# A row of norm factors by two DMA steps over memory instead of two transposes and a copy, in three of four feed-forward parts

## The reference

```
def rmsnorm(x, gain):
    y = xf * lax.rsqrt(jnp.mean(xf * xf, axis=-1, keepdims=True) + EPS)
    return y * gain
def swiglu(x, w_gate, w_up, w_down):
    return (jax.nn.silu(x @ w_gate) * (x @ w_up)) @ w_down

for l in range(2):
    x = x + 0.5 * swiglu(rmsnorm(x, ffn1_norm[l]), ffn1_w_gate[l], ffn1_w_up[l], ffn1_w_down[l])
    x = x + token_mixing(rmsnorm(x, mix_norm[l]), ...)      # three attention branches, gates, w_out
    x = x + 0.5 * swiglu(rmsnorm(x, ffn2_norm[l]), ffn2_w_gate[l], ffn2_w_up[l], ffn2_w_down[l])
```

## Time and profile before

| | us |
|---|---|
| median of 3 runs | 1146.28 (1145.64 to 1146.29) |
| profiled execution, its own time | 1145.91 |
| its span | 1144.1 |
| PE busy | 1136.0 (99%) |
| DVE busy | 777.6 (68%) |
| ACT busy | 638.4 (56%) |
| POOL busy | 70.0 (6%) |

### The profile page before, as it was taken

The page is one execution under the profiler, slowest core; times in us unless marked ns, Lnnn a source line. Parts: engine busy times, 40 slices in busy tenths (PEclk is TensorE's granted clock), DMA queues, the critical chain, the costliest instruction groups (busy, mean ns, idle before and its releaser), DMA issues.

```text
span 1144.1 us, 16114 instructions
## 1 busy us (share of the span) xinstructions
PE 1136.0 (99%) x5963; PEld 962.9 (84%) x5963; DVE 777.6 (68%) x1054; ACT 638.4 (56%) x942; POOL 70.0 (6%) x79
## 2 busy tenths in 40 slices
PE   8999999999999999999999999999999999999998
PEld 6888888888778888888888888888877788888887
DVE  4776656778677676566676756668677695766655
ACT  6545545656783565455555545556577745555542
POOL 3020000211000000000020200002110000000000
PEclk9999999999999999999999999999999999999999
DMA  9956554555354665555566556536445545656620
GB/s 310 307 192 202 183 186 146 175 170 172 124 170 148 221 221 184 185 194 197 174 166 236 184 184 190 194 99 217 148 149 161 207 142 189 222 189 196 193 85 37
DMA packets 138364, 207.34 MB, mean 181 GB/s; under 512 B 6818, under 2 KB 99028, under 8 KB 138292
## 3 DMA queue, kind: packets, MB, share of 16 engines
q1 hardware_dynamic: 137444, 205.55, 54.8%
q0 software_dynamic: 752, 0.79, 0.9%
q10 hardware_dynamic: 96, 0.02, 0.0%
HBM read 205.29 MB, written 1.05 MB: 180 GB/s over the span
## 4 chain that ended last, share of the span: by engine, by line
PE 95%; DVE 2%; ACT 1%; DMA 1%; DVEq 1%; issue 0%; SPq 0%; ACTq 0%
PE bank L526 27%; PE bank L493 16%; PE bank L497 16%; PE bank L496 16%; PE bank L530 15%; PE bank L507 1%; PE bank L720 1%; DMA raw<-in_ffn_w_up 1%; ACT probs L1018 1%; PE bank L693 1%; PE bank L741 1%; PE bank L709 0%; PE bank L708 0%; DVE w_low L1118 0%; DVE probs L1329 0%
## 5 line engine op out<-in xcount | busy, mean ns | idle before, releaser
L1118 DVE TENSOR_TENSOR w_low<-raw,w_high 128x1024 fp32r<-128x1024 f32 x388 | 472.3, 1236 | 281.6 <-ACT w_high L869 281.3
L869 ACT ACTIVATE w_high<-raw 128x1024 fp32r<-128x1024 f32 x388 | 402.0, 1055 | 317.5 <-PE bank L493 112.4
L526 PE MATMUL bank<-xT,w_high 128*128 128x512 f32 x1392 | 339.8, 391 | 0.2 <-DVE xT L1136 0.2
L526 PEld LDWEIGHTS bank<-xT,w_high 128*128 128x128 f32 x1392 | 255.4, 188 | 49.7 <-DVE xT L1136 0.7
L530 PEld LDWEIGHTS bank<-xT,w_low 128*128 128x128 f32 x1408 | 180.9, 191 | 7.4 <-issue 0.6
L530 PE MATMUL bank<-xT,w_low 128*128 128x256 f32 x1408 | 185.1, 283 | 0.4 <-DVE w_low L1118 0.4
L493 PE MATMUL bank<-w_high,xT 128*128 128x512 f32 (+1 forms) x448 | 174.4, 389 | 0.2
L497 PE MATMUL bank<-w_low,xT 128*128 128x512 f32 (+1 forms) x448 | 171.3, 382 | 0.0
L496 PE MATMUL bank<-w_high,xT 128*128 128x512 f32 (+1 forms) x448 | 171.1, 382 | 0.0
L493 PE MATMUL bank<-w_high,oT_high 128*128 128x512 f32 x416 | 162.3, 390 | 0.0
L497 PE MATMUL bank<-w_low,oT_high 128*128 128x512 f32 x416 | 161.9, 389 | 0.0
(11 more groups left out here) (129 smaller groups left out, 743.8 us busy)
## 6 DMA issues: line engine op xcount, KB each, us to landing
raw<-in_w_in SPq DMA_DIRECT2D x92, 512.0 KB, 4.5
raw<-in_ffn_w_down SPq DMA_DIRECT2D x88, 512.0 KB, 4.2
raw<-in_ffn_w_gate SPq DMA_DIRECT2D x87, 512.0 KB, 4.1
raw<-in_ffn_w_up SPq DMA_DIRECT2D x87, 512.0 KB, 5.0
raw<-in_w_out SPq DMA_DIRECT2D x16, 512.0 KB, 4.4
raw<-in_w_branch_c SPq DMA_DIRECT2D x8, 512.0 KB, 4.1
raw<-in_w_branch_a SPq DMA_DIRECT2D x4, 512.0 KB, 3.9
raw<-in_w_branch_b SPq DMA_DIRECT2D x4, 512.0 KB, 6.0
```

Source lines behind the costliest of these rows:

```text
L526: return nc.tensor.matmul(bank[b0 + n][:, :], w_high[:, slot, column(k, n)], xT[:, k], start=k == 0, stop=k == KB - 1)
L869: act.activation(w_high[:, slot], raw[:, in_slot, (p % 2) * 1024:(p % 2) * 1024 + 1024], ACT.Copy).then_inc(sem["high_ready"], 1)
L1118: dve.tensor_tensor(w_low[:, slot], raw[:, FILL_SLOT[p // 2], (p % 2) * 1024:(p % 2) * 1024 + 1024], w_high[:, slot].bitcast(F32), ALU.sub ...
```

## The change

In the first feed-forward part of the first layer nothing changes (it is called cold; its semaphores have other names). In the other three, PE makes no transposes of the factors and has no wait for the row. ACT instead sends the two columns of norm_scale, 128 values of 4 bytes each, to a line of 256 values in device memory (`send_line`, two DMAs, at the start of `ffn_chunks`, after a wait for norm_ready), and later (`send_row`, at the place of copy_row) waits for both to land and loads the line 128 times, once into each partition, as `norm_row` (128 KB in all). DVE waits for that DMA before `scale_gate` of the part's first chunk.

```diff
--- before.py
+++ after.py
@@ -100,7 +100,7 @@
     "pair_used": PAIRS, "high_ready": PAIRS, "low_ready": PAIRS,
     "blocks_turned": 18, "blocks_high": 18, "blocks_low": 18,
     "gate_done": 2 * CHUNKS, "gate_up_done": 2 * CHUNKS, "gate_summed": 2 * CHUNKS, "gate_scaled": 2 * CHUNKS, "silu_ready": 2 * CHUNKS, "hidden_ready": 2 * CHUNKS,
-    "hidden_high": 2 * CHUNKS, "hidden_low": 2 * CHUNKS, "up_summed": 2 * CHUNKS, "rest_copied": 4 * CHUNKS, "row_turned": 2, "row_ready": 2,
+    "hidden_high": 2 * CHUNKS, "hidden_low": 2 * CHUNKS, "up_summed": 2 * CHUNKS, "rest_copied": 4 * CHUNKS, 
     "product_done": 24, "residual_done": 12, "merged": 8,
     "squares_ready": 3, "norm_ready": 3,
     "proj_done": len(PROJ), "proj_read": len(PROJ), "head_squares": 4, "head_totals": 5, "heads_scaled": 5, "tables_ready": 1, "rope_done": 4,
@@ -161,6 +161,7 @@
         work = sb("work", [P, 2048])
         silu, hidden, gate_scaled, up_sum = (work[:, 512 * n:512 * n + 512].rearrange("p (f s) -> p f s", f=2) for n in range(4))
         norm_row = sb("norm_row", [P, S])
+        norm_line = nc.dram_tensor("norm_line", (1, S), F32, kind="Internal").ap()
         qk_raw = [work[:, 1024 * b:1024 * b + 1024].rearrange("p (t c) -> p t c", t=HALVES) for b in range(2)]
         merged = work[:, :].rearrange("p (t c) -> p t c", t=HALVES)
 
@@ -196,6 +197,10 @@
         x_loaded = [ctx.enter_context(nc.semaphore(f"x_loaded{cols}")) for cols in range(2)]
         first_landed = ctx.enter_context(nc.semaphore("first_landed"))
         rows_loaded = ctx.enter_context(nc.semaphore("rows_loaded"))
+        cold_row_turned = ctx.enter_context(nc.semaphore("cold_row_turned"))
+        cold_row_ready = ctx.enter_context(nc.semaphore("cold_row_ready"))
+        line_landed = ctx.enter_context(nc.semaphore("line_landed"))
+        row_landed = ctx.enter_context(nc.semaphore("row_landed"))
         trig_loaded = ctx.enter_context(nc.semaphore("trig_loaded"))
         params_loaded = ctx.enter_context(nc.semaphore("params_loaded"))
         constants_ready = ctx.enter_context(nc.semaphore("constants_ready"))
@@ -255,6 +260,10 @@
         def banks_split(stage, group, n):
 
             return BANKS_BEFORE[stage] + 2 * group + n + 1
+
+        def rows_before(layer, before):
+
+            return 2 * layer + (1 if before else 0)
 
         def value(name, layer, k):
 
@@ -601,7 +610,7 @@
                 for half in range(HALVES):
                     last = nc.tensor.transpose(bank[0][:, half * P:half * P + P], norm_scale[:, half:half + 1].to_broadcast([P, P]),
                                                ident[:, :])
-                last.then_inc(sem["row_turned"], 1)
+                last.then_inc(cold_row_turned, 1)
 
             def warm(count):
 
@@ -637,7 +646,8 @@
                 gate_up_pair(layer, first + 1, 1, chunks_before + 1)
                 pe.wait_ge(sem["blocks_low"], value("blocks_low", layer, banks_split(stage, 1, 0)))
                 gate_up_pair(layer, first + 2, 2, chunks_before + 1)
-                turn_row(layer, 3 if chunks_before else 1)
+                if not turned:
+                    turn_row(layer, 1)
                 pe.wait_ge(sem["blocks_low"], value("blocks_low", layer, banks_split(stage, 1, 1)))
                 gate_up_pair(layer, first + 3, 3, chunks_before + 1)
 
@@ -653,7 +663,8 @@
                     for n in range(2):
                         wide_pair(layer, p + 4 + n, oT_high, oT_low, 2 * j + n, opens and n == 0, i * 12, release=1 - n)
 
-                pe.wait_ge(sem["row_ready"], value("row_ready", layer, 2 if chunks_before else 1))
+                if not turned:
+                    pe.wait_ge(cold_row_ready, 1)
                 chunk(0, 0, True)
                 chunk(0, 1, False)
                 for i in range(1, (CHUNKS - 1) // 2):
@@ -913,10 +924,21 @@
                 for p in pairs[2:]:
                     high(layer, p)
 
-            def copy_row(layer, n):
-
-                act.wait_ge(sem["row_turned"], value("row_turned", layer, n))
-                act.activation(norm_row[:, :], bank[0][:, 0:S], ACT.Copy).then_inc(sem["row_ready"], 1)
+            def copy_cold_row():
+
+                act.wait_ge(cold_row_turned, 1)
+                act.activation(norm_row[:, :], bank[0][:, 0:S], ACT.Copy).then_inc(cold_row_ready, 1)
+
+            def send_line(layer, before):
+
+                act.wait_ge(sem["norm_ready"], value("norm_ready", layer, 3 if before else 1))
+                for half in range(HALVES):
+                    act.dma_start(norm_line[0:1, half * P:half * P + P].rearrange("o p -> p o"), norm_scale[:, half:half + 1]).then_inc(line_landed, 16)
+
+            def send_row(layer, before):
+
+                act.wait_ge(line_landed, 16 * HALVES * rows_before(layer, before))
+                act.dma_start(norm_row[:, :], norm_line[0:1, :].to_broadcast([P, S])).then_inc(row_landed, 16)
 
             def copy_rest(layer, chunk):
 
@@ -938,6 +960,9 @@
 
             def ffn_chunks(layer, first, before):
 
+                cold = rows_before(layer, before) == 0
+                if not cold:
+                    send_line(layer, before)
                 act.activation(sink_exp_of[0][:, 0:1], zero[:, 0:1].bitcast(F32), ACT.Silu)
                 act.drain()
                 for i in range((CHUNKS - 1) // 2):
@@ -945,8 +970,10 @@
                         p = first + 4 + 6 * j
                         for n in range(6):
                             if n == (ROW_AT if i == 0 and j == 0 else SILU_AT):
-                                if i == 0 and j == 0:
-                                    copy_row(layer, 2 if before else 1)
+                                if i == 0 and j == 0 and cold:
+                                    copy_cold_row()
+                                elif i == 0 and j == 0:
+                                    send_row(layer, before)
                                 copy_rest(layer, i * 2 + (before + 1 + j))
                                 silu_gate(layer, i * 2 + (before + 1 + j))
                             high(layer, p + n, i * 12, i)
@@ -1178,7 +1205,10 @@
                         for n in range(6):
                             if n == (ROW_AT if i == 0 and j == 0 else SILU_AT):
                                 if i == 0 and j == 0:
-                                    dve.wait_ge(sem["row_ready"], value("row_ready", layer, 2 if before else 1))
+                                    if rows_before(layer, before):
+                                        dve.wait_ge(row_landed, 16 * rows_before(layer, before))
+                                    else:
+                                        dve.wait_ge(cold_row_ready, 1)
                                 scale_gate(layer, i * 2 + (before + 1 + j))
                                 multiply_hidden(layer, i * 2 + (before + 1 + j))
                             low(layer, p + n, i * 12)
```

## The result

The changed kernel takes 1173.57 us (median of 5 runs, 1173.29 to 1175.3) against 1146.12 before (5 runs): ratio 1.0246, 95% interval 1.0235 to 1.0257. It is 27.5 us slower, where no difference that can be told was forecast. The span of the profiled run is 1171.7 us instead of 1144.1.

The account below looks back on a forecast made before the run. PE, busy 1136.0 of 1144.1 us, was taken to bound the kernel. Three parts gain 0.19 us each and the DMAs cost 0: 1146.28 - 0.57 = 1145.7 us, range 1144.9 to 1147.7.

Parts of the forecast that it names:

- The line's landing: Second line DMA, issued at about 398.0, lands in 2.0 us; ACT asks at 402.1, so 4.1 us would do.
- The right rival: Line's 4-byte writes land 6 us after issue, so the row is 1.0 us late in two parts: 1147.7; chance 0.04.
- The row's landing: Row's DMA, issued by ACT at 402.1, lands in 2.3 us, at 404.4; DVE may be held 0.1 us.
- The part of layer 1: Row's DMA can go at about 585.1, with 3.5 us without delay, 4.5 with the room; counted as nothing.
- The two bounds: Landing times of line and row: upper bound 6.8 us for each, from the slowest POOL load beside SP's fills.
- DVE's wait passes in full through silu and j = 2, and 1.0 us of it is free: Delay of DVE at L1153 reaches PE through silu and j = 2's low half, after 1.0 us of room.
- What PE gains, 0.19 us per part: Two transposes leave PE's stretch of 2.11 us, which then takes 1.92; three parts give 0.57 us.
- ACT's two issues, 0.86 us: ACT issues two line DMAs at 0.43 us each; its later work shifts by 0.86 and PE does not feel it.
- ACT issues the row only when the high halves are through: High halves of j = 0 and j = 1 end at 402.08; ACT asks for the line and issues the row at 402.1.
- The price of PE's wait: Per part with the table load, row's landing after issue less 3.1 us; for layer 1, landing less 4.5.
- my rival of a row landing at 6.8 us: Row at POOL's worst holds DVE at L1153: 9.7 us lost, 1155.4; row late by over 1.4 us per part, chance 0.06.
- The Trainium skill's sentence on a write's receipt: Fixed DMA cost near 2.0 us, mostly the receipt; the long-delay warning was set aside since output stores land in 2.0 us.

Follow-up runs that it names:

- probe2: Kernel of its own, all layers left out: single DMAs of 13 forms, each waited for; 128 writes of 4 bytes in a row land in 8.2 us.
- line_spread: Changed kernel with the line's values written 64 bytes apart and the row read from a line filled once at the start; 1145.92 us, ratio 0.9998.
- gap3: Kernel before, with six small adds delaying DVE ahead of its first work on the bank in the three parts, no new DMA; 1152.04 us, ratio 1.0050.
- pairs8: Changed kernel with one line DMA of 128 pieces of 8 bytes instead of two, row kept in that order; 1145.35 us, ratio 0.9993.
- at4: Changed kernel with scale_gate and its followers behind the fourth pair in the three parts, DMAs left as they are; 1155.32 us, ratio 1.0078.
- line_unwaited: Kernel before, transposes kept, plus the two line DMAs in each of three parts, line never read; 1146.19 us, ratio 1.0000.

## Why the prediction was wrong, by its own steps

- *The line's landing, 2.0 us.* This is the step that failed. The second line DMA, the one that ACT waits for, was to land 2.0 us after its issue and landed 8.8 to 10.0 us after it (one alone: 8.2), so that ACT waited 6.2 to 6.3 us where I had "ACT does not wait". I took the store to the output as the nearest row because both go to memory; it writes pieces of 2 KB, and no DMA of the kernel before has its data in pieces of 4 bytes. The right rival stood there ("256 writes of 4 bytes in their own descriptors have no row near them"), with 6 us, 1147.7 and a chance of 0.04.
- *The row's landing, 2.3 us.* 2.9 alone, 4.7 to 6.1 here. POOL's 2.8, also one row sent to all partitions, was the better of my two neighbours. The rest goes with the first failure: issued 6 us later than forecast, the row ran beside SP's fills (5.3 us in `probe2`); how much the fresh line adds is open.
- *The part of layer 1, counted as nothing.* It lost most, 9.4 us. And even with the line spread out, POOL's loads beside it made the line and the row slow enough for a wait of PE of 0.6 us (`line_spread`), where the forecast had the row's DMA going out at 585.1 with a room of 4.5 us.
- *The two bounds were never put together.* Both steps at my own upper bound, 6.8 us, give 398.0 + 6.8 + 6.8 = 411.6, DVE held 7.3 us, PE 6.3: some 1158 from the two parts with a table load, and 1164 if layer 1 does the same. The range ended at 1147.7, so it was narrower than the unknowns that I had written down.
- *DVE's wait passes in full through silu and j = 2, and 1.0 us of it is free.* Right: 1.0 by `gap3`, 1.1 in the changed kernel; PE's wait names DVE's w_low as forecast.
- *What PE gains, 0.19 us per part.* Right in the trace (1.92 and 1.91 us for 2.11), below what the times can tell.
- *ACT's two issues, 0.86 us.* Right: 0.84, and nobody waited for the later high halves.
- *ACT issues the row only when the high halves are through.* Wrong: in `pairs8` the DMA goes out at 400.44, before the second high half starts at 400.75. So ACT asks for the line earlier than at 402.1, and the line has less than the 4.1 us of the forecast to land; for the result it made no difference.
- *The price of PE's wait* left out the clock. Behind each wait of 7 us PE worked for 3.5 to 4.9 us at the lower clock, which cost 1.7 to 2.3 us; some 6 of the 27.5 us. PE's clock never fell in the trace before behind its start, so no row gave this price. In `at4` it also fell behind a wait of 2.4 us and not behind two of 1.7, in `gap3` not behind three of 1.7. So my rival of a row landing at 6.8 us, which makes PE wait 3.7 us, was probably priced too low as well.
- The Trainium skill's sentence on a write's receipt that can be "surprisingly long" when the target is HBM (DMA: Bandwidth & Descriptors, "Anatomy of one DMA", told there of DMAs from GpSimd) I had weighed as not borne out. For this form of write the trace agrees with it: the packets are over by 400 us and the landing is told up to 8.8 us later. It agrees for no other form: 1.4 us for the same bytes further apart. That the receipt is what takes the time no run shows. The same page's rule against a strided last dimension ("Rules for kernel authors", one descriptor per element) does not tell the two forms apart here: both go out in 288 packets, and the one whose values lie together in memory took 8.2 us, the one with gaps 1.4.

## What to carry to other kernels

If an operation has no row of its own kind in the trace (here: pieces of 4 bytes), a row that shares only its target is no measure; keep the upper bound of every unmeasured step and add them up along a chain before choosing the range. Small writes that turn a column into a line in memory should be laid at least 32 bytes apart or joined to pieces of 16 bytes (measured with 128 of them); even with pieces of 8 bytes the two steps together took 6.9 to 7.2 us in `pairs8`, which has to be covered by other work. And where PE, which never waited, is made to wait for 2.4 us or more, its clock can be a second price.

## What the runs showed that I had not expected

- 128 writes of 4 bytes into 512 bytes in a row: 8.2 us; 16 bytes apart 2.4; 32 and more apart 1.4.
- The packets of such a DMA are recorded within 1 us of each other, and the landing is told 5 to 9 us behind them.
- While it is under way SP's loads of 512 KB land in 6.4 and 7.3 us (`line_unwaited`) or 7.0 and 8.2 (changed kernel) instead of 3.9 and 6.1 before; with the values 64 bytes apart 3.9 and 4.8.
- One place read 128 times costs 0.9 us more than 128 places (2.9 against 2.0 us for 128 KB), hardly depending on the size.
- A row read from a line written just before took 4.6, 4.3 and 3.0 us in `pairs8`, from an old line at almost the same moment 2.8, 4.8 and 2.9 in `line_spread`. Why `pairs8` is slower in the first part, and whether the writing causes it, stays open.
